# A third pair of weight slots in the second round of the down projection, and its difference chunks loaded from GpSimd's queue

## The reference, cut to what matters

```python
h2 = rms_norm(x, g_ffn_pre[i])
u = causal_dwconv(h2 @ w_up[i], conv_w[i], conv_b[i])
ug, uv = u[..., :D_FF], u[..., D_FF:]
f = (jax.nn.gelu(ug, approximate=True) * uv) @ w_down[i]     # 512 x 2816 by 2816 x 1024
x = x + rms_norm(f, g_ffn_post[i])
```

## Time and profile before

| | us |
|---|---|
| median of 3 runs | 1828.74 (1826.79 to 1829.85) |
| the profiled execution | 1827.23 |
| its span, first to last instruction | 1825.4 |
| TensorE busy with matmuls | 1809.3 (99%) |
| VectorE busy | 1190.9 (65%) |
| ScalarE busy | 935.3 (51%) |
| GpSimd busy | 346.0 (19%) |
| mean granted TensorE clock | 0.996 of full speed |
| DMA, mean over the span | 139 GB/s |

### The profile page before, as it was taken

The page is one execution under the profiler, slowest core; times in us unless marked ns, Lnnn a source line. Parts: engine busy times, 40 slices in busy tenths (PEclk is TensorE's granted clock), DMA queues, the critical chain, the costliest instruction groups (busy, mean ns, idle before and its releaser), DMA issues.

```text
span 1825.4 us, 26834 instructions
## 1 busy us (share of the span) xinstructions
PE 1809.3 (99%) x9111; PEld 1506.8 (83%) x9111; DVE 1190.9 (65%) x1800; ACT 935.3 (51%) x1660; POOL 346.0 (19%) x314
## 2 busy tenths in 40 slices
PE   9999999999999999999999999999999999999998
PEld 8888888788888888887898888887888888888877
DVE  4756555555577777886656565555455887778874
ACT  4676546533454444555547764466334444445563
POOL 1002001132023334301010020012221244332010
PEclk9999999999999999999999999999999999999999
DMA  6322354479424333685253224545893333337842
GB/s 185 77 82 82 100 115 121 117 192 281 133 80 119 109 118 112 215 286 187 91 150 88 65 82 113 106 130 123 208 275 92 101 109 117 113 116 252 276 143 92
DMA packets 312392, 253.43 MB, mean 139 GB/s; under 512 B 65092, under 2 KB 265440, under 8 KB 312032
## 3 DMA queue, kind: packets, MB, share of 16 engines
q1 hardware_dynamic: 301160, 222.51, 40.6%
q0 software_dynamic: 10752, 29.36, 7.2%
q10 hardware_dynamic: 376, 0.21, 0.1%
HBM read 236.76 MB, written 42.47 MB: 153 GB/s over the span
## 4 chain that ended last, share of the span: by engine, by line
PE 95%; DMA 2%; DVE 2%; issue 0%; ACT 0%; DVEq 0%; POOL 0%; POOLq 0%; ACTq 0%; SPq 0%
PE psum L888 85%; PE psum L1203 2%; DMA raw<-in_w_down_dram 2%; PE psum L1184 2%; PE psum L1169 2%; PE psum L931 1%; PE psum L1156 1%; PE psum L1155 1%; DVE dn_wl L1981 0%; PE psum L1181 0%; PE psum L1166 0%; PE psum L1395 0%; DVE raw L2066 0%; PE psum L1165 0%; DVE dn_ll L1981 0%
## 5 line engine op out<-in xcount | busy, mean ns | idle before, releaser
L888 PE MATMUL psum<-xnh,wh 128*128 128x512 f32 (+1 forms) x1424 | 564.1, 396 | 0.0
L888 PE MATMUL psum<-xnh,wl 128*128 128x512 f32 (+1 forms) x1424 | 548.9, 385 | 0.0
L888 PE MATMUL psum<-xnl,wh 128*128 128x512 f32 (+1 forms) x1424 | 548.3, 385 | 0.0
L1514 ACT ACTIVATE wh<-raw 128x1024 fp32r<-128x1024 f32 (+2 forms) x276 | 284.6, 1033 | 495.3 <-PE psum L888 454.6
L1981 DVE TENSOR_TENSOR wl<-raw,wh 128x1024 fp32r<-128x1024 f32 (+2 forms) x276 | 364.5, 1322 | 150.1 <-ACT wh L1514 149.9
L888 PEld LDWEIGHTS psum<-xnh,wl 128*128 128x128 f32 x1424 | 267.6, 188 | 54.3
L888 PEld LDWEIGHTS psum<-xnh,wh 128*128 128x128 f32 x1424 | 269.1, 189 | 50.1 <-issue 2.7
L888 PEld LDWEIGHTS psum<-xnl,wh 128*128 128x128 f32 x1424 | 268.3, 188 | 46.9
L2219 DVE CUSTOM_DVE_ANT_0 Sp<-psum,ptok 128x128 f32<-128x128 f32 (+3 forms) x128 | 62.8, 491 | 108.4 <-issue 60.3
L2734 POOL TENSOR_TENSOR merged<-merged,th 128x512 f32<-128x512 f32 x32 | 46.8, 1463 | 265.8 <-DVE th L2351 265.7
L2431 DVE TENSOR_TENSOR ub<-psum,rb 128x512 f32<-128x512 f32 x88 | 60.6, 688 | 39.9 <-PE psum L888 39.9
(11 more groups left out here) (333 smaller groups left out, 3477.8 us busy)
## 6 DMA issues: line engine op xcount, KB each, us to landing
raw<-in_w_up_dram SPq DMA_DIRECT2D x88, 512.0 KB, 3.8
raw<-in_w_gate_dram SPq DMA_DIRECT2D x48, 512.0 KB, 3.8
col_sums<-in_w_down_dram POOLq DMA_DIRECT2D x44, 512.0 KB, 8.4
raw<-in_w_down_dram SPq DMA_DIRECT2D x44, 512.0 KB, 4.8
raw<-in_w_in_dram SPq DMA_DIRECT2D x30, 512.0 KB, 3.7
raw<-col_sums SPq DMA_DIRECT2D x22, 512.0 KB, 4.4
qspill<-f_sums SPq DMA_DIRECT2D x22, 384.0 KB, 4.8
q_raw<-qspill SPq DMA_DIRECT2D x22, 384.0 KB, 5.4
```

The costliest lines, as they stand in the source:

```text
L888: ins = pe.matmul(out, left, right, start=start and n == 0, stop=stop and n == 2)
L1514: act.activation(halves(c)[0][:, 0:n], raw[s][:, 0:n], ACT.Copy).then_inc(w_hi.sem, 1)
```

## The change

The second round gets a third pair of slots. Pairs 0 to 7 now rotate over near slots 0 and 1, the ring, and new near slots 2 and 3, which lie in the part of the first round's activations that is dead once that round ends. `near_free` says after which chunk a near slot is free: its chunk before, or for slots 2 and 3 the end of the first round. The load of a diff chunk leaves SyncE's program; GpSimd issues all 11 in a row after its last `features_apart` and ahead of `down_roots`, each with the same wait as before (`lo` of the chunk four before it). Their landings are counted by two semaphores of their own, for odd and even pairs. VectorE's `diff` waits for those.

```diff
-DN_NEAR = {ST_DOWN + n: n % DN_SLOTS - SPL for n in range(DN_TAIL_AT) if n % DN_SLOTS >= SPL}
+DN_NEAR = {ST_DOWN + n: n % DN_SLOTS - SPL for n in range(2 * PAIRS) if n % DN_SLOTS >= SPL}
+for _n in range(2 * PAIRS, DN_TAIL_AT):
+    if (_n // 2 - PAIRS) % 3 != 1:
+        DN_NEAR[ST_DOWN + _n] = _n % 2 + (_n // 2 - PAIRS) % 3
...
+def near_free(c):
+
+    before = [b for b in DN_NEAR if b < c and DN_NEAR[b] == DN_NEAR[c]]
+    if before:
+        return before[-1] + 1
+    return ST_DOWN if DN_NEAR[c] < 2 else ST_DOWN + 2 * PAIRS
...
+    diff_in = [Tally(sem(f"diff_in{i}"), 16 * len(range(i, PAIRS, 2))) for i in range(2)]
...
-               for i in range(DN_SLOTS - SPL)]
+               for i in range(2)]
...
+    dn_near += [(here("dn_wh2", 37, [P, 1024], F32R), here("dn_wl2", 82, [P, 1024], F32R)),
+                (here("dn_wh3", 41, [P, 512], F32R), here("dn_wl3", 86, [P, 512], F32R))]
...
-    N_DMA = [{"first": 3, "qC": 2, "uqn": 4, "uqp": 8, "ukn": 2, "ukv": 2, "dn_rows": 2}.get(k, 1) for k, _ in CHUNKS]
+    N_DMA = [{"first": 3, "qC": 2, "uqn": 4, "uqp": 8, "ukn": 2, "ukv": 2, "dn_rows": 2, "dn_diff": 0}.get(k, 1) for k, _ in CHUNKS]
...
+            if CHUNKS[c][0] == "dn_diff":
+                return
...
-                act.wait_ge(w_used.sem, w_used.at(L, max(c - DN_SLOTS + 1, ST_DOWN)))
+                act.wait_ge(w_used.sem, w_used.at(L, near_free(c)))
...
-            dve.wait_ge(w_landed[s], LAND[L * NCH + ST_DOWN + 2 * PAIRS + 2 * j + 1])
+            dve.wait_ge(diff_in[j % 2].sem, diff_in[j % 2].at(L, 16 * (j // 2 + 1)))
...
             features_apart(L, PAIRS - 1)
+            for j in range(PAIRS):
+                c = ST_DOWN + 2 * PAIRS + 2 * j + 1
+                pool.wait_ge(w_lo.sem, w_lo.at(L, c - RAW + 1))
+                for dst, move in chunk_dmas(L, c):
+                    pool.dma_start(dst, move).then_inc(diff_in[j % 2].sem, 16)
             down_roots(L)
```

## The result

| | us |
|---|---|
| kernel before, median of 9 runs on the same chip | 1829.85 |
| changed kernel, median of 9 runs | 1834.30 (1832.60 to 1834.83) |
| ratio, 95% interval | 1.0025 [1.0016, 1.0034] |
| the profiled executions, before and changed | 1827.23 and 1832.69 |

The change makes the kernel slower by 4.5 us; 7 us faster was forecast. The page's first line, against the earlier trace rows: TensorE is busy for 1.1 us more, and GpSimd has 22 instructions more, its DMA issues.

A forecast was written before the change was run, and what follows sets the result against it. TensorE was taken as the bound, waiting for cols 10 behind a chain of four landing buffers. Shorter waits (4.8 us) and one clock drop (2.5) gave 7.3 us off the 1828.7 median: 1821 us, range 1815.3 to 1832.

The forecast's parts named there:

- What bounds the kernel: Down projection, last three pairs: TensorE waits for late cols 10 and then runs slow; 13.4 us can be won.
- Part 1: Third slot pair: hi of cols 2 stops waiting for TensorE; 0.56 us gained in the first layer, nothing in the second.
- GpSimd's issues at nothing: GpSimd's 22 added load issues, 0.75 to 1.2 us each, are hidden in its idle time and cost nothing.
- the waits are the same ones: Diff loads issued from GpSimd wait for the same things as before, so no cost was counted for this.
- x = 4.5: Time from issue to landing of a diff chunk from GpSimd's queue, taken as 4.5 us, between 3.5 and 5.7.
- the sum: TensorE's start with cols 10: 821.9 + 4x first layer, 1726.5 + 4x second; 4.8 us gained together, 7.3 with clock.
- both clock losses: TensorE's matmuls slowed behind the waits for cols 10, one stretch per layer: 2.66 and 2.33 us lost.
- the rival of no difference: Diff landings stay at 4.9 us or a little more, waits and clock losses stay: 1826 to 1829 us, chance 0.25.
- The chain of the even pairs alone: Load, landing, subtraction, lo and next load of even diffs set cols 10's time; odd pairs' similar chain was nearly in time.
- One clock drop to go: Remaining waits of 1.6 and 2.0 us lie around the 1.6 us drop point; one of two drops goes, 2.5 us.
- The slow queue: GpSimd's software queue lands diffs slower, x = 5.7, and the chain multiplies it: 1833.5 us, chance 0.20.

The follow-up runs named there:

- e8: Kernel before, all loads on SyncE's queue, plus two landing buffers; cols and diffs use six in plain turn from cols 4 on: 1818.20 against 1829.98 us.
- e1: Changed kernel with only the third pair of slots kept, diff chunks loaded by SyncE's queue again: 1828.90 us against 1830.01 for the kernel before.
- e4: The changed kernel run once more, unaltered, as a control: 1835.71 us against 1830.01 for the kernel before.
- e2: Changed kernel with only the loads from GpSimd's queue kept, slots as in the kernel before: 1834.62 us against 1830.01 for the kernel before.
- e7: Kernel before, all loads on SyncE's queue, plus two landing buffers for diff 4, 5, 8 and 9, issued earlier: 1823.32 against 1829.49 us.
- e9: Six landing buffers used in plain turn, but all diff chunks loaded from GpSimd's queue: 1822.97 us against 1829.98 for the kernel before.

## Why the prediction was wrong, point by point

- **What bounds the kernel: right.** The chain of load, landing and lo through four buffers held the end of the round, and 13.4 us were to be won. e8 took 13.2 in the stage and 11.8 in the kernel's time. (The matmul spacing of the prediction, 7.74 / 34, is 0.228 and not 0.227, which changes nothing.)
- **Part 1, 0.56 us from the third slots: wrong, nothing to be seen.** It followed VectorE only up to the wait that went, not to the landing wait behind it (e1).
- **GpSimd's issues at nothing: right for their length, wrong for their start.** They take 0.72 to 0.84 us each, at or just under the low end of the earlier trace rows, and nobody waits for GpSimd; the first root follows the eleventh at 839.87, far ahead of its need. But "the waits are the same ones" left out that GpSimd's issue begins 0.30 us after lo has ended and SyncE's 0.09. Over the three turns this puts TensorE's start with cols 10 0.6 us back in each layer.
- **The landing time, x = 4.5: this step failed, in two ways.** First in its size. The ordinary landing is 4.9 us and not 4.5: over diff 5 to 10 the means of three GpSimd kernels (changed, e4, e2) average 4.91, of two SyncE kernels 4.89, of the ScalarE kernel 4.91. The prediction took the value of a copy to memory in a quiet stretch and supposed that a queue of its own would save something. With 4.9 the sum gives 821.9 + 19.6 = 841.5 in the first layer and 1746.1 in the second, only 1.6 us gained in the two layers together and both clock losses kept, which is the rival of no difference. Second in its form. One x for all loads left out the load that takes 6.2 to 7.0 from this queue. In the first layer of the changed kernel the four landings of the chain took 21.3 us instead of 4 x 4.5 = 18.0.
- **The chain of the even pairs alone: this let the second error through.** Diff 3 is an odd diff. VectorE takes all in one order, so 2 us on diff 3 are 2 us on diff 4 (issued 813.36, taken up 819.88, 6.5 later) and on everything behind. From there the prediction's own form holds: 844.06 + 1.93 = 845.99 for TensorE's start with cols 10, to the hundredth. Against the 839.9 of the sum that is 6.1 us late: 3.3 from the four landings, 0.6 from GpSimd's later issues, and 2.2 because diff 4 went out at 813.36 and not at 811.2. Of these 2.2, 1.0 is the whole round, which began at 805.33 instead of 804.33; in e1, without a load from GpSimd, it began at 805.88, so this part can't be laid on the queue.
- **One clock drop to go: wrong, with its premise.** The waits grew, and both drops stayed. In e7, where waits of 1.8 and 2.2 us were left, there was none.
- **The rivals.** The slow queue gave 1833.5 and 1834.3 came; its price and side came out, its mechanism did not, so that the number agrees is luck: not every landing is slower, one is, and each issue starts 0.21 us later. The Trainium skill's rule (DMA: Bandwidth & Descriptors, "Rules for kernel authors"), that DMAs spread over more issuing engines gain issue time and no bandwidth, agrees with the equal 4.9 us in all three queues. Its first-byte figures ("Specifications" there) don't show in these means, which begin at the issue; the 0.21 us lie before it.

Another page of the Trainium skill offers a cause for diff 3. SBUF — State Buffer, "SBUF: two separate sides", says that VectorE in certain modes keeps GpSimd from writing its descriptors. The rows speak against it as the difference. Behind the issue of diff 3 and behind that of diff 5 VectorE is equally busy, 2.00 of 2.00 us (third pair of numbers), both issues take 0.72, and one lands after 6.52, the other after 4.16:

```profile
809.80:811.80 2.00, 2.00 (x11) 1.65 (x10) 2.00 (x4) 0.63 (x1) 0.72 (x1) 1.00 0.87 264
```

```profile
820.20:822.20 2.00, 2.00 (x10) 1.67 (x9) 2.00 (x3) 1.54 (x4) 0.72 (x1) 1.00 0.52 172
```

The DMA share does differ, 0.87 against 0.52, but that doesn't decide it either. Behind the issue of diff 6, from the same queue, it is 0.89, and diff 6 landed in 4.60:

```profile
823.20:825.20 2.00, 2.00 (x11) 1.65 (x10) 0.78 (x2) 0.00 (x0) 0.72 (x1) 1.00 0.89 283
```

Why diff 3 is the late one stays open.

## What to carry to other kernels

Where an engine waits for landings in a chain of few buffers, a landing time taken from another place in the program is not good enough to decide the sign; look at how many loads are in flight, and cut the chain (more landing buffers in dead memory, used in plain turn) rather than change the queue. On an engine that works in one fixed order the worst landing counts and not the mean, and it counts for both chains. When loads in such a chain move to another queue, add the time from the end of what they wait for to the issue, once for each turn. Before a wait is booked as a gain, name the next wait behind it and when that one's data was issued.

## What was not expected of the hardware

- Three queues, one landing time: 512 KB landed in 4.9 us on average from SyncE's, ScalarE's and GpSimd's queue, while an issue took 0.38, 0.37 and 0.72 us and began 0.09, 0.03 and 0.30 us (medians) after the end of the lo that it waited for.
- Diff 3 from GpSimd's queue took 6.2 to 7.0 us in all eight layers in which it was issued in the plain order (changed, e4, e2, e9), and 4.3 to 4.7 from the two others. The trace has 16 completions for each such load. In the changed kernel 14 of the 16 are there 5.0 and 4.6 us after the issue, the last two at 6.0 and 6.5, and at 5.6 and 6.6. In e4 and e2 four to six of the 16 come after more than 5.3 us, in e9 one comes after more than 6.
- Landings over 6 us are not GpSimd's alone: in e8, where six loads from SyncE's queue went out within 4.4 us, three of them in each layer took 6.7 to 7.6.
- With waits of 3.2 and 3.6 us TensorE fell to its lower clock level, and its matmuls ran at it for 5.8 and 5.1 us; with two waits of 2.9 and 2.5 us a moment apart it fell as well, and with one of 1.8 or 2.2 us (e7) it did not.
